# Context squares within the first feed-forward, weight loads one place further ahead, first attention scores within v's projection

## The reference, cut to what matters

```python
def first_block(...):                       # 512 tokens + 16 meta tokens
    u = rms_norm(h, norm_mix_w)             # attention with forgetting, gated recurrence
    ...
    h = h + mixed
    u = rms_norm(h, norm_ffn_w)
    h = h + (silu(u @ w_ffn_gate) * (u @ w_ffn_up)) @ w_ffn_down
    return rms_norm(h, norm_final_w)[:, N_META:]

def second_block(x, c, ctx, c_ctx, ...):    # x is the first block's result
    for i in range(2):
        mod = silu(cond) @ ada_w[i] + ada_b[i]          # for tokens and for context
        xn = modulate(rmsnorm(h, norm_mix[i]), shift, scale)
        xc = modulate(rmsnorm(hc, norm_mix[i]), ...)
        i == 0: y, yc = diff_attention(xn, xc, ...)          # q, k with rotation; 8 heads of 2 maps
        i == 1: y = neighbourhood_attention(xn, xc, ...)     # 16 heads, table of biases
        h = h + g_m * y
        h = h + g_f * swiglu(modulate(rmsnorm(h, norm_ffn[i]), ...))
        # for i == 0 the same for the context hc
    return rmsnorm(h, norm_final)
```

## Time and profile before

| | before |
|---|---|
| median of 3 runs | 2790.52 us |
| the profiled execution | 2790.24 us, span 2788.3 us |
| TensorE matmul busy | 2572.1 us (92%) |
| weight load, beside it | 2191.3 us (79%) |
| VectorE, ScalarE, GpSimd busy | 1527.7, 1089.5, 310.4 us |
| mean granted clock | 0.963 |
| chain that ended last | TensorE 75%, VectorE 12%, ScalarE 7%, issue 4%, DMA 1% |

### The profile page before, as it was taken

The page is one execution under the profiler, slowest core; times in us unless marked ns, Lnnn a source line. Parts: engine busy times, 40 slices in busy tenths (PEclk is TensorE's granted clock), DMA queues, the critical chain, the costliest instruction groups (busy, mean ns, idle before and its releaser), DMA issues.

```text
span 2788.3 us, 36546 instructions
## 1 busy us (share of the span) xinstructions
PE 2572.1 (92%) x14635; PEld 2191.3 (79%) x14635; DVE 1527.7 (55%) x2832; ACT 1089.5 (39%) x1885; POOL 310.4 (11%) x184
## 2 busy tenths in 40 slices
PE   7988888999997999997799999998799998799998
PEld 6787777878886877776688888888688787677877
DVE  3565556657747677777744443436355556533334
ACT  5544534122234655555411212114466556322223
POOL 2222100000022221220000000002123221000001
PEclk9999999999998999999899999999899999899999
DMA  4112033535521111110233333331322221222331
GB/s 117 46 39 54 16 106 121 174 120 182 170 81 46 39 39 39 39 39 31 68 106 114 102 118 106 103 123 25 77 52 59 54 63 46 72 95 76 102 95 60
DMA packets 247330, 223.82 MB, mean 80 GB/s; under 512 B 36916, under 2 KB 215898, under 8 KB 247162
## 3 DMA queue, kind: packets, MB, share of 16 engines
q1 hardware_dynamic: 247162, 221.49, 26.4%
HBM read 219.24 MB, written 2.22 MB: 79 GB/s over the span
## 4 chain that ended last, share of the span: by engine, by line
PE 75%; DVE 12%; ACT 7%; issue 4%; DMA 1%; POOL 0%; SPq 0%; DVEq 0%; POOLq 0%; ACTq 0%
PE ps L357 23%; PE ps L358 22%; PE ps L359 22%; DVE FR L521 2%; ACT FR L516 1%; PE ps L2628 1%; ACT whi L382 1%; DVE hT L2418 1%; PE ps L646 1%; PE ps L1065 1%; ACT FA L2342 1%; PE ps L2257 1%; PE ps L2639 1%; DVE hT L2752 1%; DVE FA L2447 1%
## 5 line engine op out<-in xcount | busy, mean ns | idle before, releaser
L357 PE MATMUL ps<-Uh,whi 128*128 128x512 f32 (+2 forms) x2512 | 900.2, 358 | 38.5 <-DVE Ul L462 8.1
L358 PE MATMUL ps<-Ul,whi 128*128 128x512 f32 (+2 forms) x2512 | 884.5, 352 | 0.0
L359 PE MATMUL ps<-Uh,wlo 128*128 128x512 f32 (+2 forms) x2512 | 883.1, 352 | 0.0
L357 PEld LDWEIGHTS ps<-Uh,whi 128*128 128x128 f32 x2512 | 485.9, 193 | 113.9 <-issue 37.6
L359 PEld LDWEIGHTS ps<-Uh,wlo 128*128 128x128 f32 x2512 | 484.1, 193 | 62.5
L358 PEld LDWEIGHTS ps<-Ul,whi 128*128 128x128 f32 x2512 | 485.6, 193 | 59.0
L382 ACT ACTIVATE whi<-raw 128x1024 fp32r<-128x1024 f32 (+2 forms) x205 | 296.4, 1446 | 566.9 <-PE ps L359 552.1
L393 DVE TENSOR_TENSOR wlo<-raw,whi 128x2048 fp32r<-128x2048 f32 (+2 forms) x121 | 248.6, 2055 | 310.9 <-ACT whi L382 310.7
L357 PE MATMUL ps<-FR,whi 128*128 128x512 f32 (+1 forms) x864 | 305.4, 354 | 24.9 <-DVE FR L521 20.1
L358 PE MATMUL ps<-FR,whi 128*128 128x512 f32 (+1 forms) x864 | 302.2, 350 | 0.0
L359 PE MATMUL ps<-FR,wlo 128*128 128x512 f32 (+1 forms) x864 | 302.0, 350 | 0.0
(11 more groups left out here) (318 smaller groups left out, 3234.4 us busy)
## 6 DMA issues: line engine op xcount, KB each, us to landing
FA<-in_ada_w_dram SPq DMA_DIRECT2D x192, 256.0 KB, 2.9
raw<-in_ffn_w_gate_up_dram SPq DMA_DIRECT2D x44, 1024.0 KB, 5.2
raw<-in_ffn_w_down_dram SPq DMA_DIRECT2D x24, 768.0 KB, 4.7
raw<-in_w_in_dram SPq DMA_DIRECT2D x29, 512.0 KB, 3.9
raw<-in_da_wqkv_dram SPq DMA_DIRECT2D x24, 512.0 KB, 3.8
raw<-in_na_wqkv_dram SPq DMA_DIRECT2D x24, 512.0 KB, 3.9
raw<-in_w_ffn_gate_dram SPq DMA_DIRECT2D x11, 1024.0 KB, 5.4
raw<-in_w_ffn_up_dram SPq DMA_DIRECT2D x11, 1024.0 KB, 5.4
```

The costliest lines, as they stand in the source:

```text
L357: e.matmul(out, ah, bh, start=start, stop=False)
L358: e.matmul(out, ah, bl, start=False, stop=False)
L359: return e.matmul(out, al, bh, start=False, stop=stop)
```

## The change

- `mixed_scalar` makes the high part of the up weights after normalization block 3; f0's first gate step makes none. The context's squares and sums move to the step after the gate of the second pair in the first slice.
- In the tails of f0 and f1 the halves of the second attention chunk come after "ones", with planned delays of 1.3 and 2.2.
- Two of the tail's buffers, `st_r2` and `st_acc2`, lie elsewhere, so that the rope table's place is free earlier.
- `diff_sync` and `near_sync` begin with a fetch instead of a wait for the normalization. Before the rope stands a wait for f0's last low part; before the first bias table one for the low part of the tail's last chunk; the wait for the normalization stands before the second bias table.
- In d the rotation of k follows that of q; in d and n the first scores stand between the two parts of v's projection.

```diff
-        self.st_r1, self.st_r2, self.st_acc2 = FA[:, 4096:4608], FA[:, 4608:5120], FA[:, 5120:5632]
+        self.st_r1, self.st_r2, self.st_acc2 = FA[:, 4096:4608], FA[:, 6656:7168], FA[:, 6144:6656]
@@ mixed_scalar
         context_scalar(K, e, w, (0, 7, 1, 2, 3, 4, 5, 6)[c])
+        if c == 3:
+            split_hi(K, e, w)
@@ ffn_steps
             yield "gate", s, q, 0, m
+            if f.kind == "double" and (s, q) == (0, 1):
+                yield "squares", 0, 0, 0, 0
@@ ffn_scalar
         if what == "gate":
-            split_hi(K, e, w)
+            if m or f.kind != "double":
+                split_hi(K, e, w)
+        elif what == "squares":
+            context_squares(K, e, w)
@@ ffn_vector
+        elif what == "squares":
+            context_vector(K, e, w)
@@ tail_steps
+    yield "ones", last, 0
     if f.kind != "final":
-        yield "split", 0, 1
-    yield "ones", last, 0
+        yield "split_last", 0, 1
@@ tail_sync
     fetch_chunk(K, e, w)
     fetch_chunk(K, e, w)
+    if f.kind == "double":
+        w.wait_ge(*K.at("f_lo", f.st, sum(ns // 2 for ns in SLICES) * len(f.tiles) - 1))
@@ diff_steps
     yield "rot", 0, "q"
+    yield "rot", 0, "k"
     yield "split_first", 0, "k"
     yield "v", 0, 0
-    yield "rot", 0, "k"
+    yield "scores", 0, 0
     yield "v", 0, 512
     yield "turn_v", 0, 0
-    yield "scores", 0, 0
@@ diff_sync
-    w.wait_ge(*K.at("norm_lo", "d", KC - 1, 1))
+    fetch_chunk(K, e, w)
     e.dma_start(K.rope, K.A["rope"]).then_inc(*K.dma("rope_in"))
@@ near_sync
-    w.wait_ge(*K.at("norm_lo", "n", KC - 1, 2))
+    fetch_chunk(K, e, w)
+    w.wait_ge(*K.at("wlo_dve", K.chunk_of["n_start"] - 1))
     for what, j, x in near_steps():
         if what == "table":
             w.wait_ge(*K.was("n_max", j - 2, 3, 1))
+            if j == 1:
+                w.wait_ge(*K.at("norm_lo", "n", KC - 1, 2))
```

More of the change, by code:

```diff
@@ L1878, in tail_after @@
         ones = [("root", 0.1)] + [("second", 3.0)] * (f.kind == "double") + [(("hi", c), start + 0.5 + pace * c) for c in blocks if f.kind != "final"]
-        return {"open": (("open", 0.0),), "split": (("split", 0.0),), "tail": (("square", 0.6),), "ones": ones, "turn": (("turn", 0.1),)}
+        return {"open": (("open", 0.0),), "split": (("split", 0.0),), "split_last": (("split", 1.3),), "tail": (("square", 0.6),), "ones": ones, "turn": (("turn", 0.1),)}
     if engine == "vector":
@@ L1887, in tail_after @@
             ones += [(("keep", c), start + 9.0 + 0.5 * c) for c in blocks]
-        return {"open": (("open", 0.0),), "split": (("split", 0.5),), "tail": (("add", 0.1),), "ada_end": (("ada_end", 0.1),),
+        return {"open": (("open", 0.0),), "split": (("split", 0.5),), "split_last": (("split", 2.2),), "tail": (("add", 0.1),), "ada_end": (("ada_end", 0.1),),
                 "ones": ones, "turn": (("turn", 0.1),)}
@@ L2562, in near_tensor @@
     held = {}
+    K.named("n_start")
     for what, j, x in near_steps():
@@ L2619, in near_tensor @@
             w.wait_ge(*K.at("n_in_lo", "q", j, 0))
+            w.wait_ge(*K.at("n_in_lo", "k", j, 0))
             w.wait_ge(*K.at("n_in_lo", "k", j, 512))
@@ L2852, in scalar_program @@
     mixed_scalar(K, e, w)
-    context_squares(K, e, w)
     ffn_scalar(K, e, w, f0)
@@ L2872, in vector_program @@
     mixed_vector(K, e, w)
-    context_vector(K, e, w)
     ffn_vector(K, e, w, f0)
```

## The result

| | before | after |
|---|---|---|
| median of 4 runs | 2789.4 us (2786.2 to 2791.2) | 2768.1 us (2764.6 to 2768.6) |
| ratio, 95% interval | | 0.9922 [0.9905, 0.9939] |
| profiled execution, span | 2790.2, 2788.3 us | 2768.6, 2766.7 us |

A second set of the same kernel, six runs, gave 2765.7 us (2758.9 to 2772.1), ratio 0.9920 [0.9905, 0.9935]. The forecast was 2771, its range 2764 to 2780.

The account below looks back on a forecast made before the run. TensorE is busy nearly everywhere, so only its idle and half-clock time can be won; gains 2.5 + 1.1 + 0.9 + 6.1 + 6.0 + 2.5 = 19.1 us, taken from 2790.2, gave 2771.1, stated as 2771, range 2764 to 2780.

Parts of the forecast that it names:

- (a): First feed-forward entry: earlier high half of up weights, later context squares, end TensorE's idle before up matmuls; gain 2.5 us.
- (b): Tails: later halves of k's weights shorten the wait for the sum; 1.1 us in neighbourhood entry, 0 in differential entry.
- (c): Weight loads fetched one further ahead: gain 0.9 us in second feed-forward, 6.1 in neighbourhood entry including faster clock.
- (d): First scores moved inside v's projection in both attention entries: gain 6.0 us in the neighbourhood, 2.5 in the differential.
- (e): Rope load and first bias table go earlier, second sums' buffers move; all in time, cost 0.
- (d) near: Neighbourhood entry: first scores inside v's projection fill TensorE's idle time, 5.0 us plus 1.0 of clock; gain 6.0.
- (d) diff: Differential entry: scores moved inside v's projection, less 1.5 us new idle before k's rotation; gain 2.5 us.
- The clock rival: Differential entry: two close idle stretches drop the clock, v's matmuls take some 3 us more; 2774 us, chance 0.15.
- The bias tables: Rival, neighbourhood loop: later bias tables come too late, some 2795 us at 14 us later; chance 0.08; 8 us slack expected.

Follow-up runs that it names:

- u_squares: Kernel after with the early high half of the up weights and the later context squares and sums undone; 2775.2 us.
- u_tail: Kernel after with the halves of k's weights put back ahead of the sum of squares in the first tail alone; 2765.1 us.
- u_loads: Kernel after with the earlier weight loads undone: SP waits for the normalization's end again, one fetch less ahead; 2779.4 us.
- m_mask: Kernel after with GpSimd's mask on the first bias table held back until VectorE made the low halves of v's weights and the next chunk; 2765.7 us.
- m_order: Kernel after with ScalarE's scaling ahead of the copies of transposed v in both attentions, and VectorE's scaled sum earlier in the differential one; 2756.4 us.
- u_near: Kernel after with the first scores of the neighbourhood attention put back behind the transposes of v; 2781.1 us.

## Why the prediction was right, and where it wasn't

The time was in the range and 3 us from the forecast. The terms were not all right, and that the total came so near is in part luck. Read at each place in the profiles, the edits gave (a) 5.8, (b) 1.1 and -1.1, (c) 1.1 and 5.0, (d) 6.3 and -1.7: 16.5, where the sum had 19.1. The profiled execution gained 21.6. The other 5 are half clock that came or went in stages with the same code; the sum had no term for it.

**(a), 2.5 forecast.** Right in mechanism, too small: it was 5.8. The high half moved ahead of block 4 and the low half met TensorE in time. I priced the idle time and forgot the seven matmuls at half clock that followed it (446.35 to 449.61), another 1.6. In (c) I had counted just that. The second stretch at half clock, at 507.40, I had not foreseen at all. The 2.50 was itself a matter of clock: u_squares has 3.80. Of the table load: none was added, there are ten loads before and after. The Trainium skill ("ScalarE: Activation LUTs", section "Table sets: the hidden batching unit") says that cheap functions stand in every set; it doesn't name the square among them. The trace fits it, since squares run between two activations of line 1741 without a load.

**(b), 1.1 and 0.** The first was exact: the wait for GpSimd's sum is 5.10. The second failed. "VectorE is filled without gaps, whatever the order" was true behind the roots and false ahead of the sum, where it had 1.2 us to spare; the low half left free time for busy time. Cost 1.1, outside my bound of 0.7; u_tail shows it.

**(c), 6.1 in the neighbourhood entry and 0.9.** The transfer was the cause (u_loads: 6.6), and v runs at clock 1.00. The wait went from 3.74 to 1.12 and not to 0, so 5.0 came of the 6.1. The 0.9 of the second feed-forward came as 1.1, but u_loads didn't bring it back. The failed step is (e): "the first bias table goes earlier, cost 0". Its mask landed on VectorE's half of v's weights; m_mask shows it. I had checked that the table was not late and not what its new time runs beside.

**(d) near, 6.0.** Right. Idle time of 7.43 became 2.00 (2.4 forecast), the first transposes come 7.2 us after the first scores (7.5 forecast), and undoing it costs the stage 6.3.

**(d) diff, 2.5.** This step failed: 2.5 were forecast as gain, and the order cost 1.7 in the profile and 0.9 on the mean of seven. The wait of 1.56 before the second rotation came as forecast. From the end of the first scores to the first transposes I put 8.5; it was 10.2 (872.79 to 883.02). I had put the scaled sum behind the maxima, and that came. I had missed that the scaling could start at 876.26 and stood behind the copies of the transposed v, which wait for TensorE, until 877.77, and that the sum, so delayed, would meet GpSimd's low half. m_order shows both.

**The clock rival** (0.15, 2774) happened in its place, beside the forecast: v's first matmuls ran at half. That the total didn't come to 2774 is no merit of the sum. Half clock went in (a) and in v of the neighbourhood entry (2.3), and stages that no edit touches changed by themselves: mixers 1.7 faster, the loop of d 2.0, the loop of n 2.5, and the third feed-forward 2.9 slower. The second feed-forward with its tail fell by 3.4, of which 1.1 are (b), 1.1 stand at the wait of the earlier trace rows, and 1.6 are half clock that u_squares and u_tail still have. For all these clocks I have no cause.

**The bias tables** were in time with the slack forecast. One sum on their side was wrong: at 14 us later each of seven rounds would lose 14 less the 8.2 of slack, 5.8, and the time would be near 2812, not 2795. Nothing here came near it.

## What to carry to other kernels

When work is moved earlier, ask what it runs beside in its new place, not only whether it is late: three of the losses here were a VectorE instruction that met GpSimd or a row of VectorE that was already full. Price an idle stretch of TensorE with the slow matmuls behind it. Compare stages cut close to the edit, not totals: stages with the same code differed by up to 10 us between profiles, while the stretch around (a) agreed within 0.3. When a planner's delays order the engines, look for the step that is ready and stands behind one that waits: hoisting two such steps won about as much (4.2 and 1.5 us in their stages) as moving the scores.

## What the runs showed of the hardware

**VectorE and GpSimd hold each other up.** Three VectorE instructions that take two inputs from SBUF were stretched, each by a little less than what was left of the GpSimd instruction: the low half 2.71 instead of 1.23 (it started at 1940.27, GpSimd ended at 1941.89), the scaled sum 2.63 instead of 1.02 (880.33, 882.14), a half of the rotated q 1.77 instead of 0.69 (866.46, 867.68). The maxima at 879.46, which read PSUM, kept their 0.95 beside the same GpSimd instruction that stretched the scaled sum. It works the other way too. In the timelines of VectorE and GpSimd of the kernel after, GpSimd's second addition takes 2.12 instead of 1.27; it started at 865.56, inside VectorE's half that ended at 866.55:

```profile
862.80 1.27 POOL L2485 TENSOR_TENSOR FA<-FA 128x512 f32<-128x512 f32 x1 [25.14 <-DVE FA L2407]
...
865.33 1.22 DVE L393 TENSOR_TENSOR wlo<-raw,whi 128x1024 fp32r<-128x1024 f32 x1
...
865.56 2.12 POOL L2485 TENSOR_TENSOR raw<-raw,FA 128x512 f32<-128x512 f32 x1 [1.48 <-DVE FA L2407]
...
866.46 1.77 DVE L523 SCALAR_TENSOR_TENSOR FR<-FA,FR 128x512 fp32r<-128x512 f32 x1
```

The Trainium skill ("SBUF — State Buffer", section "SBUF: two separate sides") calls the port pair of the two engines an exclusive lock, held for the whole instruction by the one that starts first. The trace agrees: GpSimd's end at 1941.89 and a half of 1.23 is 1943.1, and it ended at 1942.98.

**The clock after the same wait differs from run to run.** In the nine profiles with 1.56 us between the rotations the second rotation ran at half clock in five (0.76 or 0.77 us) and at full in four (0.47), all behind the same 2.2 us before the first or less. In three of the four full ones the half clock came in v right behind; only u_tail had none before the first scores. In the four profiles without this second wait none stood between the first rotation and the first scores. So the second wait goes with the half clock, but it isn't its whole cause: in after and u_near the first rotation ran at half already (0.77), before the second wait, behind 2.2 us of idle time as in ten others where it ran at full.
